# Retention and attention merged into one program, and another order of weighting and turning between feed-forward and projections

## What is computed

```
x = layer_norm(ALPHA * x + g2 * swiglu(...), ln2_w, ln2_b)      # end of block one
h = rms_norm(x, norm_mix)                                       # x / sqrt(mean(x*x) + eps) * norm_mix
proj = h @ w_in                                                 # split into r_q r_k r_v r_g d_q d_c d_pe d_g i_q i_k i_w
ret = head_group_norm(retention(r_q, r_k, r_v), ret_norm) * silu(r_g)
dsa = sparse_attention(d_q ..., top 256 keys by an index score) * silu(d_g)
x = x + concat([ret, dsa]) @ w_out
```

## Time and profile before

| | |
|---|---|
| median of 3 runs | 2206.23 us (2204.26 to 2206.43) |
| the profiled execution's own time | 2204.3 us |
| its span | 2202.5 us |
| mean granted TensorE clock | 0.971 of full |
| busy: TensorE, VectorE, ScalarE, GpSimd | 94%, 57%, 34%, 20% of the span |
| instructions | 27774 |

### The profile page before, as it was taken

How to read it: one execution, slowest core, us unless ns; L and a number is a source line. 1 busy time by engine, 2 the same in 40 slices (tenths; PEclk the granted TensorE clock), 3 DMA queues, 4 the chain that set the end, 5 groups by cost and what they waited for, 6 DMA issues and landing times. The chain is left out here.

```text
span 2202.5 us, 27774 instructions
## 1 busy us (share of the span) xinstructions
PE 2077.9 (94%) x10549; PEld 1562.1 (71%) x10549; DVE 1257.1 (57%) x2133; ACT 746.3 (34%) x1380; POOL 432.5 (20%) x472
## 2 busy tenths in 40 slices
PE   7999999996999999999999998889999887989998
PEld 3844474475888888888888887756888664658876
DVE  6582695467963333224543225479999777761433
ACT  2222112153123232224443224355221334760425
POOL 2910001142300000000000002224667351300110
PEclk9999999997999999999999999999999998999999
DMA  8543120113243332353343232112211002013101
GB/s 318 169 126 115 38 77 1 30 49 132 89 144 91 100 96 79 98 157 105 115 125 110 85 99 85 53 49 72 58 48 48 28 1 77 1 47 127 39 0 77
DMA packets 195977, 184.83 MB, mean 84 GB/s; under 512 B 13246, under 2 KB 166142, under 8 KB 192538
## 3 DMA queue, kind: packets, MB, share of 16 engines
q1 hardware_dynamic: 192890, 172.85, 25.3%
q0 software_dynamic: 2880, 10.49, 1.3%
q10 hardware_dynamic: 96, 0.02, 0.0%
HBM read 169.37 MB, written 12.64 MB: 83 GB/s over the span
## 5 line engine op out<-in xcount | busy, mean ns | idle before, releaser
L1911 DVE TENSOR_TENSOR ff_part<-ff_raw,ff_part 128x1024 fp32r<-128x1024 f32 (+2 forms) x150 | 162.4, 1083 | 415.1 <-ACT ff_part L1814 415.0
L1814 ACT ACTIVATE ff_part<-ff_raw 128x1024 fp32r<-128x1024 f32 (+2 forms) x150 | 141.9, 946 | 422.9 <-PE ps L1688 422.9
L1686 PE MATMUL ps<-h,ff_part 128*128 128x512 f32 x704 | 274.5, 390 | 0.4 <-DVE ff_lowf L1924 0.4
L1687 PE MATMUL ps<-h,ff_part 128*128 128x512 f32 x704 | 273.9, 389 | 0.0
L1688 PE MATMUL ps<-h,ff_part 128*128 128x512 f32 x688 | 267.7, 389 | 0.0
L2541 DVE TENSOR_SCALAR_CACHE_REDUCE pj_junk<-NM,prm 128x384 uint8<-128x384 f32 (+1 forms) x186 | 163.7, 942 | 1.1
L1686 PE MATMUL ps<-pj_part,h 128*128 128x512 f32 x384 | 153.1, 399 | 0.2 <-ACT PJ L2398 0.2
L1686 PEld LDWEIGHTS ps<-h,ff_part 128*128 128x128 f32 x704 | 132.1, 188 | 28.1 <-issue 0.8
L1687 PEld LDWEIGHTS ps<-h,ff_part 128*128 128x128 f32 x704 | 132.2, 188 | 27.2
L1687 PE MATMUL ps<-pj_part,h 128*128 128x512 f32 x384 | 150.4, 392 | 0.0
L1688 PE MATMUL ps<-pj_part,h 128*128 128x512 f32 x384 | 150.1, 391 | 0.0
(11 more groups left out here) (606 smaller groups left out, 3983.4 us busy)
## 6 DMA issues: line engine op xcount, KB each, us to landing
ff_raw<-in_w_ffn_in SPq DMA_DIRECT2D x86, 512.0 KB, 3.7
s_wm<-in_w_mod SPq DMA_DIRECT2D x16, 1024.0 KB, 4.8
pj_raw<-in_w_in SPq DMA_DIRECT2D x64, 256.0 KB, 2.6
ff_raw<-in_w_ffn_out SPq DMA_DIRECT2D x32, 384.0 KB, 3.4
ff_raw<-in_w_ffn_out SPq DMA_DIRECT2D x32, 320.0 KB, 3.0
mod_w<-in_w_mod SPq DMA_DIRECT2D x8, 1024.0 KB, 8.9
mod_x<-in_x SPq DMA_DIRECT2D x8, 512.0 KB, 13.9
mx_spread<-mx_lfd SPq DMA_DIRECT2D x16, 256.0 KB, 3.9
```

The source lines that it names most:

```text
L1686: nc.tensor.matmul(out, w[0], x[0], start=first, stop=False)
L1687: nc.tensor.matmul(out, w[0], x[1], start=False, stop=False)
L1814: nc.scalar.activation(part[s % 2][0][:, 0:n, :], raw[s][:, 0:n, :], ACT.Copy).then_inc(hi, 1)
L1911: v.tensor_tensor(part[s % 2][1][:, 0:n, :], raw[s][:, 0:n, :], part[s % 2][0][:, 0:n, :].bitcast(F32), ALU.subtract).then_inc(lo, 1)
```

## The change

Three edits.

1. In `stage_first_end`, tiles 1 and 3 are turned into banks 6 and 7 instead of 2 and 3, and each turn waits for the subtraction of the tile that last used its pair.
2. GpSimd multiplies x2 by `norm_mix` first, from tile `t` into `h`, ahead of the store; ScalarE scales `h` by the inverse root last. The roles of `hs` and `hr` are exchanged with it. `inverse(2)` moves from in front of `norm(3)` to inside it, behind the statistics.
3. `stage_retention` becomes `retention_programs`, which returns five functions, one for each engine; `stage_retention_attention` calls each at the head of the engine's attention program, in one block. VectorE's norm is cut in two, `spread_out` (up to the variance) and `scaled` (reciprocal and product). Those of the last tile, and mask parts 1 and 2 of tile 4, move behind attention's steps 0, 1 and 2, and so do the last root and the last `lower` of ScalarE. Waits replace what the end of the block ensured; `den` and one `run` buffer get places of their own.

```diff
+    def turned(i, b):
+        return K.bank[(6 if i in (1, 3) else 2) + b]
...
             def weigh(n):
-                pool.wait_ge(hs, n + 1)
-                nc.gpsimd.tensor_tensor(h[n % 2][:], h[n % 2][:], rows[:, 2, :], ALU.mult).then_inc(hr, 1)
+                if n >= 2:
+                    pool.wait_ge(tr, 2 * n + 6)
+                nc.gpsimd.tensor_tensor(h[n % 2][:], t[n % 3][:], rows[:, 2, :], ALU.mult).then_inc(hs, 1)
...
             for n in range(NL):
                 pool.wait_ge(x2r, n + 1)
+                weigh(n)
                 pool.dma_start(K.x2[(4 + n) * P:(5 + n) * P, :], t[n % 3][:]).then_inc(stored[n % 3], 16)
-                if n:
-                    weigh(n - 1)
-            weigh(NL - 1)
...
                 for k in range(KT):
-                    if i and k % 4 == 0:
-                        pe.wait_ge(tev, 2 * i - 1 + k // 4)
+                    if i >= 2 and k % 4 == 0:
+                        before = i - 2 if i < 5 else i - 1
+                        pe.wait_ge(tev, 2 * before + 1 + k // 4)
...
-                    last = nc.tensor.transpose(K.bank[2 + k // 4][:, (k % 4) * P:(k % 4 + 1) * P], src, K.ident[:])
+                    last = nc.tensor.transpose(turned(i, k // 4)[:, (k % 4) * P:(k % 4 + 1) * P], src, K.ident[:])
...
             def scale(n):
                 act.wait_ge(rcp, n + 1)
-                if n >= 2:
-                    act.wait_ge(tr, 2 * n + 6)
-                nc.scalar.activation(h[n % 2][:], t[n % 3][:], ACT.Copy, scale=ss[:, n:n + 1]).then_inc(hs, 1)
+                act.wait_ge(hs, n + 1)
+                nc.scalar.activation(h[n % 2][:], h[n % 2][:], ACT.Copy, scale=ss[:, n:n + 1]).then_inc(hr, 1)
...
                 link(v.bn_aggr(mv, st))
+                if n == 3:
+                    inverse(2)
                 v.tensor_scalar(rs, mv[:, 1:2], LN_EPS, None, ALU.add).then_inc(sq, 1)
...
             spread(2)
-            inverse(2)
             norm(3)
...
-    run = K.at("rt_run", 192, [P, T])
+    run = [K.at(f"rt_run{n}", kb, [P, T]) for n, kb in enumerate((192, PJ_KB + 16))]
...
+            if i:
+                spread_out(i - 1)
+                scaled(i - 1)
+            if i < NT - 1:
                 mask(FIRST[1 + i // 3], i % 3)
-            norm(NT - 1)
-            mask(FIRST[3], 2)
...
-    den = K.prm[:, 0:NT * AH].rearrange("p (i h) -> p i h", i=NT)
+    den = K.prm[:, 128:128 + NT * AH].rearrange("p (i h) -> p i h", i=NT)
...
+            R.sync(sp)
+            sp.wait_ge(R.out, NT)
             for b in range(2):
+                if b:
+                    sp.wait_ge(R.gate, NT)
                 sp.dma_start(K.raw_end[b][:], I["w_out_2"][0].rearrange("(k p) n -> p k n", p=P)[:, :, b * HALF:(b + 1) * HALF]).then_inc(w_in[b], 16)
...
+            R.gpsimd(pool)
             for m in range(2 * KT):
...
+            R.tensor(pe)
+            pe.wait_ge(R.prer, 2 * NT)
+            pe.wait_ge(R.dqr, NT)
             pairs = len(steps) // 2
             logits(0)
+            pe.wait_ge(R.oev, NT)
             for pair in range(pairs):
...
+            R.scalar(act)
             expo(0)
             expo(1)
             for n in range(len(steps)):
                 take(n)
                 if n + 2 < len(steps):
                     expo(n + 2)
+                if n == 0:
+                    R.root(NT - 1)
+                elif n == 2:
+                    R.lower(4)
+                elif n == AH + KT - 1:
+                    act.wait_ge(R.done, NT)
...
                 dve.wait_ge(S["lmm"], n // 2 + 1)
+                if h == 0 and i >= 4:
+                    dve.wait_ge(R.masked, R.first.index(i) + 1)
...
+            R.vector(dve)
             logit(0)
             logit(1)
             for n in range(len(steps)):
                 if n + 2 < len(steps):
                     logit(n + 2)
                 take(n)
+                if n == 0:
+                    R.spread_out(NT - 1)
+                    R.mask(4, 1)
+                elif n == 1:
+                    R.scaled(NT - 1)
+                elif n == 2:
+                    R.mask(4, 2)
+                elif n == late[0]:
+                    dve.wait_ge(R.done, NT)
...
 STAGES = (stage_modulate, stage_s5, stage_mixers, stage_join_ffn, stage_first_end,
-          stage_project, stage_retention, stage_attention, stage_second_end)
+          stage_project, stage_retention_attention, stage_second_end)
```

More of the change, by code:

```diff
@@ L2123, in take @@
                     nc.scalar.activation(K.h3[0][:, 4 * b:4 * b + 4, i * P:(i + 1) * P],
-                                         K.bank[2 + b][:].rearrange("p (k t) -> p k t", k=4), ACT.Copy).then_inc(thi, 1)
+                                         turned(i, b)[:].rearrange("p (k t) -> p k t", k=4), ACT.Copy).then_inc(thi, 1)
             def root(n):
@@ L2573, in lower_mask, with retention_programs @@
     return K.nc.scalar.activation(x, x, ACT.Copy, scale=-LOW, bias=LOW)
-def stage_retention(K):
+def retention_programs(K):
     nc, I = K.nc, K.I
@@ L2600, in stage_retention @@
     uk = K.wsT
+    R = Kept(nc, I, None)
     names = ("zero const tr qkr dqt dqr smm prob xqr kzr out oev upd state var gate norm done chain "
@@ new lines, in vector, with spread_out, scaled, mask @@
+    def vector(dve):
+        v = nc.vector
+        link = Link(v, S["chain"])
+        def spread_out(i):
+            o = K.PJ[:, R_Q, i, :].rearrange("p (h d) -> p h d", h=RH)
+            sqr = K.PJ[:, R_K, i, :].rearrange("p (h d) -> p h d", h=RH)
+            dve.wait_ge(S["oev"], i + 1)
+            link(v.tensor_reduce(mu, o, AX.X, ALU.add))
+            link(v.tensor_scalar(mu, mu, 1.0 / RD, None, ALU.mult))
+            link(v.tensor_tensor(o, o, mu.unsqueeze(2).to_broadcast([P, RH, RD]), ALU.subtract))
+            link(v.tensor_tensor(sqr, o, o, ALU.mult))
+            link(v.tensor_reduce(var, sqr, AX.X, ALU.add))
+            v.tensor_scalar(var, var, 1.0 / RD, RMS_EPS, ALU.mult, ALU.add).then_inc(S["var"], 1)
+        def scaled(i):
+            o = K.PJ[:, R_Q, i, :].rearrange("p (h d) -> p h d", h=RH)
+            dve.wait_ge(S["var"], 2 * i + 2)
+            link(v.reciprocal(var, var))
+            v.tensor_tensor(o, o, var.unsqueeze(2).to_broadcast([P, RH, RD]), ALU.mult).then_inc(S["norm"], 1)
+        def mask(i, part):
+            last = mask_part(K, link, i, part, run[i == FIRST[3]], flag)
+            if part == 2:
+                last.then_inc(S["pick"], 1)
+                dve.wait_ge(S["pick"], FIRST.index(i) + 1)
+        dve.wait_ge(S["clear"], 1)
+        for a in range(2):
+            v.tensor_copy(spread[0:PE_D, a, 0:PE_D], K.ident[0:PE_D, 0:PE_D]).then_inc(S["spread"], 1)
+        for i in range(NT):
+            dve.wait_ge(S["turn"], i + 1)
+            v.tensor_copy(lat_pe[:, :, i * P:(i + 1) * P], K.bank[6 + i % 2][:, 0:2 * P].rearrange("p (m t) -> p m t", m=2)).then_inc(S["latr"], 1)
+        for part in range(3):
+            mask(FIRST[0], part)
+        dve.wait_ge(S["const"], 80)
+        dve.wait_ge(S["zero"], 2)
+        for i in range(NT):
+            s = i % 2
+            dve.wait_ge(S["smm"], i + 1)
+            if i >= 2:
+                dve.wait_ge(S["out"], i - 1)
+            for a in range(2):
+                pr = v.tensor_tensor(prob[s][:, :, a, :], K.bank[3 + a][:].rearrange("p (j t) -> p j t", j=J), intra[:, :, a, :], ALU.mult)
+            pr.then_inc(S["prob"], 1)
+            if i + 1 < NT:
+                new = state[1 - s]
+                if i:
+                    dve.wait_ge(S["dec"], i)
+                dve.wait_ge(S["upd"], i + 1)
+                b = K.bank[7][:].rearrange("p (j c) -> p j c", j=J)
+                for a in range(2):
+                    d = slice(RD * a, RD * (a + 1))
+                    if i:
+                        up = v.tensor_tensor(new[d, :, d], new[d, :, d], b[d, :, d], ALU.add)
+                    else:
+                        up = v.tensor_copy(new[d, :, d], b[d, :, d])
+                up.then_inc(S["state"], 1)
+                dve.wait_ge(S["state"], i + 1)
+            if i:
+                spread_out(i - 1)
+                scaled(i - 1)
+            if i < NT - 1:
+                mask(FIRST[1 + i // 3], i % 3)
+        R.spread_out, R.scaled, R.mask = spread_out, scaled, mask
@@ L2859, in stage_attention, with stage_retention_attention @@
+    R.sync, R.gpsimd, R.tensor, R.scalar, R.vector = sync, gpsimd, tensor, scalar, vector
+    R.out, R.gate, R.done, R.prer, R.dqr, R.oev, R.masked = (S[n] for n in "out gate done prer dqr oev masked".split())
+    R.first = FIRST
+    return R
+def stage_retention_attention(K):
     nc, I = K.nc, K.I
     J = AH // 2
+    R = retention_programs(K)
     kfT, val = K.kfT, K.val
```

390 lines of the change are left out of this document (163 added, 227 removed).

## The result

| | before | after |
|---|---|---|
| median, same chip | 2205.32 us (2204.26 to 2206.43, 4 runs) | 2190.16 us (2189.49 to 2191.51, 4 runs) |
| ratio | | 0.9932, interval 0.992 to 0.9945 |
| profiled execution, its span | 2204.3, 2202.5 us | 2190.49, 2188.7 us |
| mean granted TensorE clock | 0.971 | 0.976 |

The kernel became 15.2 us faster between the medians (0.7%), 13.8 between the two spans. The forecast was 7.5 faster and its range ended at 2193.0; the sign was right and the size half of what came.

What follows compares the result with a forecast made beforehand. It took TensorE as bounding, a stage worth shortening only where TensorE stands still or runs at low clock. Stage one -2.5 and seam -5.0 gave -7.5, so 2198.7 us against 2206.23; range 2193.0 to 2205.0.

Steps and rivals of the forecast that it cites:

- -2.5 - 5.0: The forecast's sum: stage one 2.5 us shorter and the seam 5.0 shorter, -7.5 in all.
- Part 1: Stage one's bank pairs: both early TensorE stalls go, GpSimd is late next, mix 0 ends near 1366.9, not 1370.9.
- Part 2: Stage one, weight first and scale last: walked to turn(7), the stage ends earlier, taken as -2.5 us.
- The new wait: Stage one: scale(0) on ScalarE waits for GpSimd's product, so VectorE's low(3) and norm(2) come later, a wait of 5.4 us.
- with mix 1 at full clock: Stage one's other case: turn(7) then waits for low(6), and the stage ends 3.1 us earlier instead of 2.2.
- Part 3: The seam as one program: moved VectorE work sits where TensorE waits, logits(3) starts 5.0 us earlier.
- so I take the low clock, 3.41, to 1828.2: At the seam, logits(1) after 2.7 us of idle was taken to run at the low clock, lasting 3.41.
- rival B: At the seam, logits(1) and (2) run at full clock, 1.4 back each: -11 to -13, 2194 us; chance 0.14.
- The table switches: ScalarE at the seam: two more table loads, covered by spread_out(7) and logit(3), 0 in the sum, 2.6 us if uncovered.
- rival D: Table loads on the path at the seam, take(1) and expo(3) late by 2.6: 2201.3 or 2204 us; chance 0.06.
- SP's two loads and the x2 store: SP's w_out loads leaving at 1820.2 and stage one's last store issued near 1390.1 were both to cost nothing.
- Rivals A and C: A: only the seam gains, 2201.2 to 2204, chance 0.20; C: ScalarE waits for GpSimd every tile, 2210 to 2212, chance 0.07.

Runs made afterwards that it cites:

- e3: The kernel before, unchanged, run and profiled once more: 2205.66 us, ratio 1.0006.
- e2: The kernel before with only edit 3, retention and attention as one program: 2197.31 us, ratio 0.9973.
- e1: The kernel before with only edits 1 and 2, bank pairs and weight first: 2196.85 us, ratio 0.9968.
- e7: The changed kernel with the last tile's norm, root and mask parts put back in front of the first logit pass: 2194.32 us, ratio 0.995.
- e8: The changed kernel with four more table loads in attention, by a root of one number at steps 1 and 3: 2190.27 us, ratio 0.9938.
- e11: The changed kernel with spread_out(7) ahead of attention's step 0, mask parts one step later and lower(4) two: 2188.1 us, ratio 0.9931.
- e13: The changed kernel with forty transposes of the identity on TensorE in front of logits(2): 2188.32 us, ratio 0.9931.
- e5: The kernel before with only edit 1, the bank pairs and their waits: 2201.12 us, ratio 0.9981.
- e6: The kernel before with only edit 2, weight first and scale last, all tiles in banks 2 and 3: 2197.99 us, ratio 0.9968.
- e9: The kernel before with thirty transposes of the identity on TensorE ahead of tile 6's turn: 2201.07 us, ratio 0.9986.
- e10: The changed kernel with tile 4's product between GpSimd's fourth and fifth weight difference and two ScalarE splits drawn forward: 2193.05 us, ratio 0.9951.

## Why the prediction was off by half

**The step that failed is the sum: "-2.5 - 5.0".** It had two terms, the stages that the diff touches, and took everything between them for a shift. The third was the projections, -2.3 (329.91 as the mean of before, e3 and e2; 327.59 of after, e1, e7, e8, e11, e13). The forecast had read that TensorE idles 3.50 in front of tile 6's turn and then runs at the low clock, and had ended its view of the clock with the stage. The rows 1400.23 to 1403.45 of the trace of before were there to be read, 4 us on. Had they been, the question would have been asked whether the change takes away what makes them; e5, e6 and e9 say yes for 1.5 of the 2.3, and leave open why the other 0.8, 47 us on, changed too.

Term by term:

- **Part 1, the bank pairs.** Right that both stalls go and that GpSimd's differences are late next; mix 0 ended within 0.5 of the walk. What it couldn't tell is that this part hardly counts: -2.0 of stage one alone, 0.4 beside part 2 (e5, e6, e1).
- **Part 2, -2.5.** The new wait and each start on VectorE came within 0.4 us. Measured -3.4 between the two profiles, -3.9 over all (52.52 before, e3, e2; 48.66 the six above). The size was off where I took mix 1 for as long as the old last mix, 6.8: it ran 1375.30 to 1380.80, 5.5. The working named that case, "with mix 1 at full clock", and gave it 3.1.
- **Part 3, -5.0.** The step "so I take the low clock, 3.41, to 1828.2" failed. The row it went by had 2.96 of idle, this one has 2.75, and the group ran at 1.99. That 1.4 would make -6.4 of the -5.0; measured is -6.1 against the profile that the walk went by and -6.5 over all (31.15 old, 24.6 new). That was rival B's first half. That TensorE keeps the lead held: the later groups stand in the same distances as before.
- **Terms at nothing.** The table switches (rival D) are settled by e8. SP's two loads and the x2 store delayed nothing that a row shows.
- **Rivals A and C** are out: stage one gained, turn 7 came earlier, and scale(1) to scale(3) waited 1.06 at most for GpSimd's product.

-3.9 - 2.3 - 6.5 are 12.7 of the 14.1 to 15.2 that the medians show (14.1 by e8, the same in time as the changed kernel, in a batch of its own). Attention's mean fell by 0.6 more (119.3 in the six profiles with the old seam, 118.7 in after, e2, e7, e8, e10 and e13). It is 120.2 in before and e5, which were granted 0.88 over its last 30 us, and 118.5 to 119.2 in the others, granted 0.94 to 0.95 in after, e1 and e3. The last 0.8 to 1.9 are about what two batches differ by, and stay open.

The third term could have been read from rows that were there. The clock of logits(1) could not: with 2.7 of idle either could be argued, and the range should have held both. It ended 5.7 below the forecast, and the third term and logits(1) alone are 3.7 of the 6.6 to 7.7 that were missing; stage one's 1.4 is the next.

## What to carry to other kernels

Count a stage's gain up to where the granted clock is again what it was, and not to its last instruction: list the low-clock stretches of the whole trace first, and for each ask which idle times may have made it and whether the change touches one of them. Where an engine waits for another that is itself waiting, a filler on TensorE shows how much of a stall is the stall and how much the clock behind it (e9, -3.3; in e13 its 2.4 showed in the profile and not in the medians). And when a wait on GpSimd is removed by starting it earlier, look which VectorE instructions with both operands in SBUF it now runs beside.

## What the runs showed of the hardware

- The granted clock fell 1.3 us into back-to-back matmuls (0.36 to 0.57 each at 1400.23), with 1.84 idle and a busy mix before, 12.5 us behind an idle time of 3.50. It did so in before, e3 and e2. It did not when that idle time was filled (e9) or gone (e6), nor in e5, which kept it (3.48) and had shorter early stalls (2.56 and 1.05 for 4.31 and 5.27). So waiting can be paid that far behind itself, but no single idle time was shown to set the price.
- Equal idle times don't give equal clocks: eight matmuls behind 2.75 idle at full clock (1.99, in all seven profiles with the moved work), others behind 2.65 at the low one (3.39 to 3.79 in the six profiles with the old seam); what TensorE did before the idle time differs, a dense retention in the one and a group already at the low clock in the other.
- Work that computes nothing can pay: 3.4 us of transposes made a kernel 3.3 faster (e9, ratio 0.9977 to 0.9995).
- VectorE, 5.70 for an instruction of 1.28, lost to four GpSimd instructions in a row (e10); in the changed kernel it took 1.70 beside the same kind.
